# Four of the projections of a two-block network as units of seven block products, with one gate parked in DRAM

## The chip, the cores and the metric

The kernel runs on one core of a Trainium2 chip. The metric is the device time of one execution in microseconds (us). Engines are called as the profile calls them: PE (TensorE matmuls), PEld (its weight loads), DVE (VectorE), ACT (ScalarE), POOL (GpSimd) and SP (SyncE, which issues DMAs here).

## What is computed

Two blocks follow one another on x of 1024 positions by 1024 channels, in float32. Only two places bear on the change. The first mixer ends with an output projection:

```
x = x + concatenate([a, r]) @ w_out
```

The second mixer takes six slices of one projection and mixes two branches (each of the four D x D slices below, and w_conv_out, is a 1024 by 1024 by 1024 product):

```
proj = xn @ w_in + b_in
u_ssm, c_bgate, c_cgate, c_val, g_ssm, g_conv = split(proj)
z    = gelu(s5_branch(u_ssm))                       # 512 wide
y_a  = (z @ w_glu_a) * sigmoid(z @ w_glu_b)
y_b  = (c_bgate * causal_short_conv(c_cgate * c_val, conv_w, conv_b)) @ w_conv_out
merged = sigmoid(g_ssm) * y_a + sigmoid(g_conv) * y_b
h = h + merged @ w_out
```

After it stands an MLP with a hidden width of 4096 (squared relu) and a last norm.

## The kernel before

**Numbers.** A float32 operand is cut in two parts, high and low, and each product is three matmuls: high by high, high by low, low by high. ACT makes a high part with a copy (`make_high` line 513, or `high_a`, `high_w` lines 2069 and 2077), DVE the low part with a subtraction (`make_low` line 517, `low_a`, `low_w` lines 2085 and 2091). A matmul has 128x128 weights and 512 columns.

**project()** is the plain way to multiply. A list of jobs is cut into pieces of two k-tiles. For each piece SP loads the weights, ACT and DVE cut them (two pieces may be cut ahead), PE multiplies them into 8 (or 4) PSUM banks, and the last piece of a job is emptied by ACT or DVE with what the job asks for (a bias and a sigmoid, a multiplication, an addition). A product of 1024 by 1024 by 1024 takes 8 x 2 x 8 x 3 = 384 matmuls. Beside it runs a `side`: an object whose `vector`, `scalar`, `tensor` and `sync` methods are called once per piece and put other work into the engines' queues, by a share of costs per piece (`Side.turn`). A `following` list lets the first piece of the next stage be loaded and cut before the stage ends.

**Sevens** multiplies a list of units. A unit is one 1024 by 1024 by 1024 product, cut in blocks of 512, done as seven block products of sums (table `PRODUCTS`) in place of eight: 7 x 48 = 336 matmuls. It runs in 14 pieces (two halves for each product) of 24 matmuls. The sums of activations are made by DVE (`sum`); the sums of weights are made by the DMA engines: SP loads a block into a slot (line 2042), and POOL issues loads that add further blocks to it (`load_more`, line 2047), each waiting for the one before. For each product, `take` adds the PSUM banks to the blocks that they belong to (line 2150, DVE) or copies the first of them (ACT). `square` closes a block of the MLP's hidden layer. The sum T2 is the first that needs two additions in a row (`first_sums`), and its piece is the fifth.

**The stages around the change**, each a block of instructions with a barrier of all engines at its end: in the first mixer `mix_out` (two jobs of `project`, line 2402 reloads x beside it, and `MemoryTurned` norms and turns the memory rows); in `mix_second`, after the norm and the state-space input, `m2_cv` (the two value slices, with the recurrence beside it), `m2_gates` (slices 0 and 4 and then w_conv_out, with the short convolution beside it), `m2_last` (slice 3, into the buffer of x, with the gelu of the state-space output beside it), `m2_glu` (two 512-wide products) and then `mlp`, a Sevens of nine units (w_out and the MLP). The cross attention's output, `x_out`, is a Sevens of one unit.

## Time and profile before

| | us |
|---|---|
| median of the runs (3) | 3289.81 |
| lowest and highest | 3289.38, 3291.3 |
| the profiled execution, its own time | 3289.8 |
| its span in the profile | 3288.0 |
| PE busy (matmuls) | 2982.7 |
| DVE busy | 1706.5 |
| ACT busy | 1072.1 |

The profiled execution's time is the median of the runs. A span is from the first to the last instruction. PE is the engine with the largest busy share over the whole program; the shares by stage are in the rows below.

### The profile page before, as it was taken

To read this page: it belongs to the slowest core of one execution; us is meant where nothing else is said; L and a number is where in the kernel's file an instruction comes from. 1 tells how busy PE (TensorE), PEld (TensorE's weight loads), DVE (VectorE), ACT (ScalarE), POOL (GpSimd) and SP (SyncE) were. 2 spreads that over 40 slices of the span, in tenths; PEclk is the share of its full clock that TensorE was granted. 3 is DMA by queue.
4 is the path that set the end of the run, shared out by engine and by line. 5 is a ranking of instruction groups with operands and counts; after the bars stand their busy time and mean duration, and the time that the engine had idled before them with its cause. 6 is when DMAs were issued, how large, how long until landed. Compare 5 with 4: busy or idle time off the path is not lost. (4 is left out here: it accounts for less than half of the span.)

```text
span 3288.0 us, 36352 instructions
## 1 busy us (share of the span) xinstructions
PE 2982.7 (91%) x14320; PEld 2230.5 (68%) x14320; DVE 1706.5 (52%) x2382; ACT 1072.1 (33%) x1596; POOL 309.6 (9%) x347
## 2 busy tenths in 40 slices
PE   7998777999999889877776699999999999999998
PEld 7887754656878577332222688788888788888887
DVE  4125855886253675111110863752122778787878
ACT  3442334665143441100000422102132264434344
POOL 0001012210000000111110200000000011111110
PEclk8998888999999999999998799999999999999999
DMA  3121100002131238999996423211114455656663
GB/s 99 45 52 11 11 14 1 1 1 82 60 122 59 41 68 350 419 420 421 418 414 258 184 65 56 75 51 51 39 42 119 135 114 122 122 120 127 125 132 92
DMA packets 167418, 422.50 MB, mean 128 GB/s; under 512 B 47505, under 2 KB 61457, under 8 KB 141137
## 3 DMA queue, kind: packets, MB, share of 16 engines
q1 hardware_dynamic: 129696, 346.97, 29.3%
q0 software_dynamic: 36416, 69.23, 11.3%
q10 hardware_dynamic: 1152, 4.19, 0.3%
q8 instruction: 104, 1.70, 0.2%
q14 instruction: 50, 0.40, 0.0%
HBM read 405.13 MB, written 32.83 MB: 133 GB/s over the span
## 5 line engine op out<-in xcount | busy, mean ns | idle before, releaser
L2187 PE MATMUL mlp_ps<-mlp_w_ring,mlp_a_ring 128*128 128x512 f32 x1680 | 384.1, 390 | 4.2 <-PEq L572 4.2
L2187 PEld LDWEIGHTS mlp_ps<-mlp_w_ring,mlp_a_ring 128*128 128x128 f32 x1680 | 315.9, 188 | 70.1 <-issue 4.6
L2187 PE MATMUL mlp_ps<-mlp_a_ring,mlp_w_ring 128*128 128x512 f32 x1344 | 306.4, 389 | 1.3 <-ACT mlp_normed L4554 1.3
L3400 PE MATMUL ffn_ps<-moe_wgu,moe_rowsT 128*64 128x512 f32 x1024 | 244.9, 634 | 51.4 <-issue 26.9
L2187 PEld LDWEIGHTS mlp_ps<-mlp_a_ring,mlp_w_ring 128*128 128x128 f32 x1344 | 252.0, 188 | 53.7 <-issue 1.5
L517 DVE TENSOR_TENSOR m_w_cut<-m_w_raw,m_w_cut 128x512 fp32r<-128x512 f32 (+1 forms) x79 | 72.2, 914 | 363.1 <-ACT m_w_cut L513 362.8
L2077 ACT ACTIVATE mlp_w_ring<-mlp_raw 128x1024 fp32r<-128x1024 f32 x126 | 133.6, 1060 | 341.3 <-PE mlp_ps L2187 330.3
L3436 DVE TENSOR_TENSOR moe_hid<-ffn_ps,moe_gated 128x256 f32<-128x256 f32 x32 | 13.6, 425 | 416.0 <-ACT moe_gated L3448 416.0
L2091 DVE TENSOR_TENSOR mlp_w_ring<-mlp_raw,mlp_w_ring 128x1024 fp32r<-128x1024 f32 x126 | 154.2, 1224 | 115.4 <-ACT mlp_w_ring L2077 115.0
L3400 PEld LDWEIGHTS ffn_ps<-moe_wgu,moe_rowsT 128*64 128x64 f32 x1024 | 79.2, 145 | 196.4 <-issue 169.0
L513 ACT ACTIVATE m_w_cut<-m_w_raw 128x512 fp32r<-128x512 f32 (+1 forms) x79 | 64.0, 810 | 435.4 <-PE m_gates_ps L628 190.7
L628 PE MATMUL m_cv_ps<-m_high,m_w_cut 128*128 128x512 f32 x512 | 161.9, 398 | 7.0 <-DVE m_w_cut L517 2.9
L628 PE MATMUL m_gates_ps<-m_high,m_w_cut 128*128 128x512 f32 x512 | 157.8, 389 | 1.1 <-PEq L572 1.1
L2047 POOL DMA_DIRECT2D mlp_raw<-in_w_ff_dram x80 | 96.9, 1355 | 522.8 <-DMA mlp_raw<-in_w_ff_dram 320.7
L3421 PE MATMUL ffn_logitsT_ps<-moe_wd,moe_hidT 128*64 128x512 f32 x512 | 116.9, 598 | 18.2 <-DVE moe_hidT L3442 18.2
L517 DVE TENSOR_TENSOR mix_w_cut<-mix_w_raw,mix_w_cut 128x512 fp32r<-128x512 f32 (+1 forms) x47 | 31.4, 667 | 191.2 <-ACT mix_w_cut L513 191.1
L628 PE MATMUL mix_in_ps<-mix_high,mix_w_cut 128*128 128x512 f32 x384 | 118.7, 390 | 0.1
L628 PEld LDWEIGHTS m_cv_ps<-m_high,m_w_cut 128*128 128x128 f32 x512 | 95.8, 190 | 30.1 <-DVE m_w_cut L517 8.1
L3448 ACT ACTIVATE moe_gated<-ffn_ps 128x256 f32<-128x256 f32 x32 | 12.3, 384 | 315.4 <-PE ffn_ps L3400 315.4
L628 PE MATMUL mix_in_ps<-mix_w_cut,mix_high 128*128 128x512 f32 (+1 forms) x384 | 111.3, 372 | 0.9 <-PEq L286 0.9
L628 PEld LDWEIGHTS m_gates_ps<-m_high,m_w_cut 128*128 128x128 f32 x512 | 96.0, 188 | 21.4 <-issue 1.5
L2150 DVE TENSOR_TENSOR x<-x,mlp_ps 128x512 f32<-128x512 f32 x160 | 100.4, 683 | 5.8 <-PE mlp_ps L2187 5.8
(580 smaller groups left out, 5991.5 us busy)
## 6 DMA issues: line engine op xcount, KB each, us to landing
moe_wgu<-in_moe_w_gate_dram SPq DMA_DIRECT2D x64, 1024.0 KB, 19.2
moe_wgu<-in_moe_w_up_dram SPq DMA_DIRECT2D x64, 1024.0 KB, 24.6
moe_wd<-in_moe_w_down_dram SPq DMA_DIRECT2D x64, 1024.0 KB, 25.7
mlp_raw<-in_w_ff_dram POOLq DMA_DIRECT2D x80, 512.0 KB, 6.3
mlp_raw<-in_w_ff_dram SPq DMA_DIRECT2D x64, 512.0 KB, 3.8
m_w_raw<-in_w_in_dram SPq DMA_DIRECT2D x48, 256.0 KB, 2.8
mix_w_raw<-in_w_in_dram SPq DMA_DIRECT2D x40, 256.0 KB, 2.6
m_w_raw<-in_w_in_dram SPq DMA_DIRECT2D x20, 512.0 KB, 3.7
```

The source lines that it names most:

```text
L513: nc.scalar.activation(part(s, 0).bitcast(F32R), raw(s), ACT.Copy).then_inc(high_ready, 1)
L517: nc.vector.tensor_tensor(part(s, 1).bitcast(F32R), raw(s), part(s, 0), ALU.subtract).then_inc(low_ready, 1)
L628: ins = nc.tensor.matmul(ps[:, place, :r.shape[-1]], l, r, start=(k == 0 and sw is high and wh == 0), stop=(k == job.nk - 1 and sw is low))
L2047: pool.dma_start(self.slots[slot][:, 2 * h:2 * h + 2], self.block_of(u, name, h), accum_op=ALU.add).then_inc(self.more[slot][h], 16)
L2077: self.nc.scalar.activation(self.w_part(g, 0).bitcast(F32R), self.w_slot(name, h), ACT.Copy).then_inc(self.w_high, 1)
L2091: self.nc.vector.tensor_tensor(self.w_part(g, 1).bitcast(F32R), self.w_slot(PRODUCTS[q][1], h), self.w_part(g, 0), ALU.subtract).then_inc( ...
L2150: nc.vector.tensor_tensor(at, at, ps, ALU.subtract if q in NEGATIVE else ALU.add).then_inc(self.added, 1)
L2187: ins = self.nc.tensor.matmul(self.ps[:, 4 * banks + tile], l, r, start=(opens and h == k == n == 0), stop=(h == k == 1 and n == 2), skip_ ...
L3400: ins = self.nc.tensor.matmul(self.ps_h[r, i].rearrange("p (i n) -> p i n", i=2), self.rowsT[:, i, k, r], self.wgu[:, w * self.parts + h, ...
L3421: ins = self.nc.tensor.matmul(self.ps_y[r, half], self.hidT[:, i, k, r], self.wd[:, w * self.parts + h, k, half * CH:(half + 1) * CH], sta ...
L3436: self.nc.vector.tensor_tensor(self.hid[:, b % self.small], self.ps_h[:, b % self.small, EH:], self.gated[:, b % self.small], ALU.mult).th ...
L3448: self.nc.scalar.activation(self.gated[:, b % self.small], self.ps_h[:, b % self.small, :EH], ACT.Silu).then_inc(self.gated_ready, 1)
```

## The change

Of `m2_gates` nothing stays in `project`: slices 4 and 0 and w_conv_out become three units of a new Sevens, `gates`. Slice 3 (`m2_last`) now comes ahead of them, straight after `m2_cv`; its result leaves for DRAM in four parts (`gate_kept`), because the units use its buffer. Gelu's result, cut in high and low (`z_pair_kept`), goes to DRAM too, since its place is needed. The normed input is put together again from its parts (`normed`). Beside `m2_last` run gelu, the short convolution and this addition. The sigmoid of slice 4 is parked in DRAM in four blocks (`sigmoid_kept`) and comes back into `mixed`; z and the gate come back for `m2_glu`. `mix_out` becomes a Sevens of one unit (`mixed_out`), with the reload of x in four blocks and the memory rows' turning inside it. The first piece of `mlp` is now cut inside `m2_glu`'s last job (`FirstPiece` as a side), not behind it. `hold_sem` semaphores are given back (`release`), and buffers of `mlp` lie elsewhere.

```diff
@@ Sevens
-    def square(self, dve, u, q):
-        block = [b for b, first in TAKES[q] if not first][0]
...
+    def close(self, eng, u, q):
+        for block in [b for b, first in TAKES[q] if not first]:
+            for h in range(2):
+                eng.wait_ge(self.added, self.adds[self.at(u, q)] + 2 * h + 2)
+                self.units[u].close[1](eng, block, h).then_inc(self.made, 1)
@@ run, scalar, where nothing was cut ahead
+                        if not self.started:
+                            self.high_a(act, g)
                         self.high_w(act, g)
-                        self.high_a(act, g)
+                        if self.started:
+                            self.high_a(act, g)
...
+                        if g and h == 0:
+                            was, q_was, _ = self.piece(g - 1)
+                            if units[was].close[0] == "scalar":
+                                self.close(act, was, q_was)
@@ mix_first
-            project(c, "mix_out", stream, jobs, source=hT, fetch=fetch, side=turned, tail=turned, following=kv_jobs,
-                    busy=(28, 8))
+        mixed_out(c, a, x, hT, first_home - 4 * KD * T, kv_jobs).run()
+class MemoryBeside(Beside):
+    def fetch(self, sp):
+        rows = self.a["x"][0].rearrange("(m p) d -> p m d", p=P)
+        sv = self.sevens
+        sv.begin(sp)
+        for block, sem in self.back.items():
...
+            sp.dma_start(self.x[at], rows[at]).then_inc(sem, 16)
+            if block == "11":
+                sp.wait_ge(sv.more[2][1], 32)
+                for h in range(2):
+                    sv.load(sp, 0, "B22", 3, h)
+    def tensor(self, pe, g, tile):
+        sv = self.sevens
+        if (g, tile) in ((12, 1), (12, 3)):
+            m = tile // 2
+            pe.wait_ge(sv.added, sv.added_by(0, 4, 7))
+            self.turned.turn(pe, m)
+    def opening(self, pe):
+        self.c.keep_busy(self.turned.tail_ps[:, 0], 28)
@@ the side of m2_last
+class LastGate(Gelu):
+    def vector_steps(self, dve):
+        yield from super().vector_steps(dve)
+        yield from self.convolve()
+        while self.piece < 12:
+            yield None
+        dve.wait_ge(self.z_kept, 32)
+        for k in range(KD):
+            self.c.nc.vector.tensor_tensor(self.normed[:, k], self.pair[0][:, k], self.pair[1][:, k],
+                                           ALU.add).then_inc(self.restored, 1)
+            yield 1.3
+    def keep_gate(self, sp, j):
+        sp.wait_ge(self.emptied["scalar"], 4 * (j + 1))
+        at = slice(2 * j, 2 * j + 2)
+        sp.dma_start(self.kept_gate[:, at], self.gate[:, at]).then_inc(self.gate_kept[j], 16)
@@ beside the three units
+class GatesBeside(Beside):
+    def after_loads(self, sp, u):
+        sv = self.sevens
+        if u == 1:
+            for block in FINAL:
+                sp.wait_ge(sv.made, sv.final_done(0, block, 1))
...
+                sp.dma_start(self.kept_sigmoid[at], self.gate[at]).then_inc(self.sigmoid_kept[block], 16)
+        else:
+            for block in FINAL:
+                sp.wait_ge(self.sigmoid_kept[block], 16)
+            sp.wait_ge(sv.a_low, sv.split(1, "A22", 1))
+            sp.dma_start(self.mixed[:], self.kept_sigmoid).then_inc(self.sigmoid_back, 16)
+    def sync(self, sp):
...
+        self.stream.begin(sp, self.jobs)
+        sp.wait_ge(sv.made, sv.final_done(2, "21", 1))
+        for j in range(2):
+            at = slice(4 * j, 4 * j + 4)
+            sp.dma_start(self.gate[:, at], self.last.kept_gate[:, at]).then_inc(self.gate_back[j], 16)
+    def gpsimd_end(self, pool):
+        sv = self.sevens
+        pool.wait_ge(sv.a_low, sv.split(2, "A22", 1))
+        for part, kept in zip(self.z, self.last.kept_z):
+            pool.dma_start(part[:].bitcast(F32R), kept.bitcast(F32R)).then_inc(self.z_back, 16)
@@ mix_second
             project(c, "m2_u", stream, input_job, side=parameters, following=value_jobs, busy=(0, 9))
-            project(c, "m2_cv", stream, value_jobs, banks=4, side=Recurrence(s5, parameters), following=gate_jobs)
-            project(c, "m2_gates", stream, gate_jobs, side=conv, following=last_jobs)
+            project(c, "m2_cv", stream, value_jobs, banks=4, side=Recurrence(s5, parameters), following=last_jobs)
             c.recycle(0)
-            project(c, "m2_last", stream, last_jobs, banks=4, side=Gelu(c, u[:], z, *z_pair), following=glu_jobs)
-            sevens = out_and_mlp(c, a, x, t1, residual, moved, base)
-            project(c, "m2_glu", stream, glu_jobs, fetch=sevens.begin, tail=FirstPiece(sevens))
...
+            glu_jobs[0].ready = (gates.beside.z_back, 32)
+            project(c, "m2_last", stream, last_jobs, banks=4, side=last)
+            gates.run()
+            c.recycle(0)
+            sevens = out_and_mlp(c, a, x, mixed, residual, moved, base)
+            project(c, "m2_glu", glu_stream, glu_jobs, fetch=sevens.begin, side=FirstPiece(sevens, 6, 8))
             sevens.run()
@@ gate_units: what closes a block of each unit
+    def sigmoid(act, block, h):
+        chs, t = units[0].half(block, h)
+        for ch in range(chs.start, chs.stop):
+            ins = nc.scalar.activation(gate[:, ch, t], gate[:, ch, t], ACT.Sigmoid, bias=bias[:, 4, ch:ch + 1])
+        return ins
+    def times_conv(dve, block, h):
+        chs, t = units[1].half(block, h)
+        for ch in range(chs.start, chs.stop):
+            ins = nc.vector.scalar_tensor_tensor(conv[:, ch, t], gate[:, ch, t], bias[:, 0, ch:ch + 1],
+                                                 conv[:, ch, t], ALU.add, ALU.mult)
+        return ins
+    def times_sigmoid(dve, block, h):
+        chs, t = units[2].half(block, h)
+        dve.wait_ge(beside.sigmoid_back, 16)
+        return nc.vector.tensor_tensor(mixed[:, chs, t], mixed[:, chs, t], gate[:, chs, t], ALU.mult)
@@ FirstPiece, called at piece 6 of m2_glu
+    def scalar(self, act, s):
+        sv = self.sevens
+        if s == self.at:
+            sv.high_w(act, 0)
+            act.wait_ge(sv.w_low, 1)
+            act.wait_ge(self.emptied["vector"], self.before)
+            sv.high_a(act, 0)
```

**The order that results.** First DVE in the stage `m2_last`, before (its 16 pieces of weights are cut in the rows of `m_w_cut`; `m_u_cut` are the low parts of gelu's result):

```order
L517 TENSOR_TENSOR m_w_cut<-m_w_raw,m_w_cut 128x2x256 x4
L3972 TENSOR_TENSOR m_u_cut<-m_last_side_ps,m_t_cut 128x512 x2
...
L3972 TENSOR_TENSOR m_u_cut<-m_last_side_ps,m_t_cut 128x512 x2
L517 TENSOR_TENSOR m_w_cut<-m_w_raw,m_w_cut 128x2x256 x8
L453 TENSOR_TENSOR m_w_cut<-m_w_raw,m_w_cut 128x1024
```

and DVE in the same stage with the change, from the seventh piece's cut on (`m_conv` is the short convolution):

```order
L4010 TENSOR_TENSOR m_u_cut<-m_last_side_ps,m_t_cut 128x512 x2
L4621 TENSOR_SCALAR m_conv<-m_t,m_laid 128x1024
L4624 SCALAR_TENSOR_TENSOR m_conv<-m_t,m_laid,m_conv 128x1023
L523 TENSOR_TENSOR m_w_cut<-m_w_raw,m_w_cut 128x2x256
L4624 SCALAR_TENSOR_TENSOR m_conv<-m_t,m_laid,m_conv 128x1022
L4621 TENSOR_SCALAR m_conv<-m_t,m_laid 128x1024
L4624 SCALAR_TENSOR_TENSOR m_conv<-m_t,m_laid,m_conv 128x1023
L4624 SCALAR_TENSOR_TENSOR m_conv<-m_t,m_laid,m_conv 128x1022
L523 TENSOR_TENSOR m_w_cut<-m_w_raw,m_w_cut 128x2x256
```

The 24 operations of the convolution, which stood beside `m2_gates`, now stand three or four at a time between two cuts of `m2_last`, and 8 additions to `m_normed` follow them; the cut for the stage behind is gone.

Then ACT from the last job of `m2_last` into the next stage, with the change:

```order
L519 ACTIVATE m_w_cut<-m_w_raw 128x2x256 x3
L4613 ACTIVATE x<-m_last_ps,m_laid 128x512 x4
L578 UNCONDITIONAL_BRANCH
L2263 UNCONDITIONAL_BRANCH
L2090 ACTIVATE gates_a_ring<-m_normed 128x1024
L2098 ACTIVATE gates_w_ring<-gates_raw_15059 128x1024
```

Both high parts of the first piece stand behind the barrier (the two branches); before, the last cut in `m2_last` was the next stage's first piece.

Last SP, from the loads of the third unit to the end of the stage `gates`, and POOL's queue at the same place:

```order
L2063 DMA gates_raw_15061<-in_w_conv_out_dram 128x2x512 x2
L4106 DMA m_mixed<-sigmoid_kept 128x8192
L433 DMA m_glu_w_raw<-in_w_glu_b_dram 128x2x512 x2
L4116 DMA x<-gate_kept 128x4096 x2
L2235 UNCONDITIONAL_BRANCH
```

```order
L2068 DMA gates_raw_15059<-in_w_conv_out_dram 128x2x512 x2
L2068 DMA gates_raw_15061<-in_w_conv_out_dram 128x2x512 x2
L2068 DMA gates_raw_15062<-in_w_conv_out_dram 128x2x512 x2
L4122 DMA glu_z_high<-z_pair_kept 128x4096
L4122 DMA glu_z_low<-z_pair_kept 128x4096
L2235 UNCONDITIONAL_BRANCH
```

These five large loads (4 MB of sigmoids, 4 MB of gates, 4 MB of z) are new, and so are the stores that they read.

## Rows read from the trace of the kernel before

**Rows 1.** Page: busy time and share of the span; PE's granted clock in 40 slices.

```profile
PE 2982.7 (91%) x14320; PEld 2230.5 (68%) x14320; DVE 1706.5 (52%) x2382; ACT 1072.1 (33%) x1596; POOL 309.6 (9%) x347
...
PEclk8998888999999999999998799999999999999999
```

**Rows 2.** Windows: start:end length, busy us (count) PE PEld DVE ACT POOL, clock, DMA, GB/s.

```profile
811.30:898.60 87.30, 87.30 (x386) 72.26 (x387) 30.23 (x34) 17.35 (x21) 0.00 (x0) 1.00 0.29 107
2133.00:2395.20 262.20, 262.19 (x1152) 216.07 (x1152) 85.85 (x87) 44.36 (x49) 0.00 (x0) 1.00 0.16 47
2396.30:2488.60 92.30, 91.10 (x416) 75.17 (x416) 19.97 (x24) 34.96 (x43) 0.00 (x0) 1.00 0.18 52
1144.50:1221.10 76.60, 76.40 (x336) 62.98 (x336) 60.84 (x70) 33.51 (x43) 7.22 (x6) 1.00 0.31 56
2739.00:2893.00 154.00, 154.00 (x681) 127.50 (x680) 123.26 (x129) 65.84 (x73) 25.39 (x21) 1.00 0.62 126
2581.00:2585.00 4.00, 3.87 (x11) 3.15 (x12) 2.98 (x3) 3.83 (x4) 2.40 (x2) 0.63 0.79 266
```

**Rows 3.** Timeline at mix_out's end: start us, us, engine, line, [idle before <-releaser].

```profile
898.42 1.91 PE L2507 MATMUL mix_out_ps<-ident,x_mem 128*128 128x128 f32 x16
898.62 0.69 DVE L2421 TENSOR_TENSOR x<-mix_out_ps,x 128x512 f32<-128x512 f32 x1 [0.67 <-PE mix_out_ps L628]
...
904.18 0.47 PE L628 MATMUL x_kv_up_ps<-x_w_cut,x_memT 128*128 128x512 f32 x1 [0.30 <-PEq L572]
```

**Rows 4.** Timeline from m2_last into m2_glu.

```profile
2488.59 0.69 ACT L4451 ACTIVATE x<-m_last_ps,m_laid 128x512 f32<-128x512 f32 x1 [0.67 <-PE m_last_ps L628]
...
2489.58 0.70 PE L628 MATMUL m_glu_ps<-m_t_cut,m_w_cut 128*128 128x512 f32 x2 [1.03 <-PEq L572]
```

**Rows 5.** Lines in two units of mlp: busy us, mean ns | idle before.

```profile
L2091 DVE TENSOR_TENSOR mlp_w_ring<-mlp_raw,mlp_w_ring 128x1024 fp32r<-128x1024 f32 x28 | 34.3, 1224 | 28.1 <-ACT mlp_w_ring L2077 28.0
L2077 ACT ACTIVATE mlp_w_ring<-mlp_raw 128x1024 fp32r<-128x1024 f32 x29 | 30.8, 1061 | 81.6 <-PE mlp_ps L2187 81.6
...
L2150 DVE TENSOR_TENSOR x<-x,mlp_ps 128x512 f32<-128x512 f32 x32 | 20.1, 682 | 0.8 <-PE mlp_ps L2187 0.8
...
L2160 DVE SCALAR_TENSOR_TENSOR mlp_hidden<-mlp_hidden 128x1024 f32<-128x1024 f32 x8 | 9.4, 1221 | 0.0
```

**Rows 6.** Timeline from m2_glu into mlp.

```profile
2577.67 0.69 DVE L4508 TENSOR_TENSOR m_t<-m_t,m_glu 128x512 f32<-128x512 f32 x1
2578.28 1.22 DVE L2091 TENSOR_TENSOR mlp_w_ring<-mlp_raw,mlp_w_ring 128x1024 fp32r<-128x1024 f32 x1
2579.41 1.22 DVE L2085 TENSOR_TENSOR mlp_a_ring<-m_t,mlp_a_ring 128x1024 fp32r<-128x1024 f32 x1
...
2581.13 0.76 PE L2187 MATMUL mlp_ps<-mlp_w_ring,mlp_a_ring 128*128 128x512 f32 x1 [4.22 <-PEq L572]
```

**Rows 7.** Timeline of POOL: the additions of T2 beside m2_glu.

```profile
2494.45 2.59 POOL L2047 DMA_DIRECT2D mlp_raw<-in_w_out_dram  x2 [483.23 <-DMA mlp_raw<-in_w_out_dram]
2505.06 1.20 POOL L2047 DMA_DIRECT2D mlp_raw<-in_w_out_dram  x1 [8.02 <-DMA mlp_raw<-in_w_out_dram]
```

**Rows 8.** DMA issues of 2480 to 2680 us: size, median us to landing.

```profile
mlp_raw<-in_w_out_dram POOLq DMA_DIRECT2D x10, 512.0 KB, 9.9
...
x<-residual SPq DMA_DIRECT2D x2, 2048.0 KB, 11.2
```

**Rows 9.** DMA issues in two units of mlp.

```profile
mlp_raw<-in_w_ff_dram POOLq DMA_DIRECT2D x21, 512.0 KB, 6.3
```

**Rows 10.** Timeline of DVE in m2_last: the last cut of weights of a piece.

```profile
2478.43 0.69 DVE L517 TENSOR_TENSOR m_w_cut<-m_w_raw,m_w_cut 128x512 fp32r<-128x512 f32 x1 [4.75 <-ACT m_w_cut L513]
```

**Rows 11.** Lines of 1900 to 2500 us: the short convolution.

```profile
L4461 DVE SCALAR_TENSOR_TENSOR m_t<-m_t,m_laid 128x1023 f32<-128x1023 f32 (+1 forms) x16 | 20.5, 1284 | 0.6
...
L4459 DVE TENSOR_SCALAR m_t<-m_t,m_laid 128x1024 f32<-128x1024 f32 x8 | 6.5, 810 | 0.1
```

**Rows 12.** DMA issues of 1940 to 2110 us: a large store.

```profile
s_kept<-x SPq DMA_DIRECT2D x1, 2304.0 KB, 7.0
```

331 lines of the change are left out of this document (205 added, 126 removed).

## The prediction

> **What bounds the kernel now.** I read the page first, then windows over the stages that the change touches, then the timelines at their borders. On the page PE is busy 91% of the span at close to its full clock [rows 1]; the reader should see that no other engine has half as dense a record over the whole, so a stage is priced by PE until something in it is shown to be later. The windows say it for each stage [rows 2]: m2_gates (262.2 us for 1152 matmuls) and mix_out (87.3 us) have no idle time on PE at all, m2_last 1.2 us in 92.3, and DVE fills a third of the first two and a fifth of m2_last. So in these stages time is the number of matmuls by 262.2 / 1152 = 0.2276 us. The same view holds the price of what they become: the single unit of x_out took 76.6 us for its 336 matmuls (0.228 us each), and two units in the middle of mlp ran 154.0 us without a gap, with DVE at 123 of 154 us (80%) and the clock at 1.00. A unit is thus bound by PE too, with a fifth of DVE's time left. That is the whole case for a gain: fewer matmuls at the same rate. Against it stand the borders between stages, and DMAs that did not exist.
>
> **The change, part by part.**
>
> *Products, second mixer.* Six jobs of 192 matmuls become three units of 336: 1152 - 1008 = 144 fewer, by 0.2276 = **-32.8 us**. Slice 3 and the glu products keep their count.
>
> *Products, first mixer.* 384 become 336: 48 fewer, **-10.9 us**; the window of x_out against that of mix_out says 76.6 against 87.3 [rows 2], the same within 0.2.
>
> *mix_out's end.* Before, PE's last product ends at 898.6 and the next stage starts at 904.18 [rows 3]: 5.6 us, of which 1.9 are the 16 transposes of the memory rows, the rest a chain ACT, DVE, filler matmuls, barrier. Now the transposes stand inside the unit (1.9 again), and behind the last product come one addition (0.69), one cut of the next weights (1.22) and the barrier (0.3, below): 2.2. So 4.1 in place of 5.6: **-1.5 us**. Its start I leave as it is, since 28 filler matmuls stand ahead in both.
>
> *m2_last into gates.* Stages of `project` follow one another in 1.03 us: ACT's last emptying is 0.69, from 2488.59 to 2489.28, and PE begins 0.30 later [rows 4]; 0.30 is the barrier. The first piece of gates isn't cut ahead. Behind the barrier ACT makes two high parts (1.06 each) and DVE, after the second, a low part (1.22) [rows 5]: 0.7 + 0.3 + 2.1 + 1.2, and 0.5 for SP's last store of the gate, which is issued after the last emptying, and for semaphores: 4.8 us. Against 1.0: **+3.8 us**.
>
> *gates into m2_glu.* After the last product: one addition 0.68, two closings of 1.22 (the multiplications by the conv branch's sigmoid, 1024 elements, as L2160), one cut for m2_glu 1.22 [rows 5], barrier 0.3, semaphores 0.2: 4.8 us against 1.1: **+3.7 us**.
>
> *m2_glu into mlp.* Before, two cuts of 1.22 stood between DVE's last addition and the barrier, and PE idled 4.22 us [rows 6]. They move ahead of the last job's emptying, where DVE has room: the gap falls to about 1.8, **-2.4 us**.
>
> *The clock at these borders.* After that 4.22 us gap, the 4 us from 2581 to 2585 have a granted clock of 0.63 [rows 2], a mean of the two levels: most of it was at the lower one (1.2 GHz), the rest at 2.4; 4 x 0.37 = 1.5 us lost. Gaps of 1.0 us leave it at full. So the two new gaps of 4.8 cost 1.5 each, and the one that shrinks to 1.8 gives its 1.5 back: **+1.5 us**. If the clock doesn't fall, this is 0 or -1.5; if both new stages start a whole 4 us at the lower level, +2.5.
>
> *T2 of the first unit.* In mlp the unit's first weight sum was begun in the stage ahead; in gates and mix_out it begins with the stage. Beside m2_glu the chain ran like this: stage begin 2489.5, first addition issued at 2494.45, the second, which waits for it, at 2505.06 [rows 7], 15.5 us after the begin, and landed 6.3 [rows 9] to 9.9 us [rows 8] later: 21.8 to 25.4, with the two cuts 24.1 to 27.7. PE wants it for the fifth piece: 3.5 us to start, four pieces of 24 x 0.2276 = 5.46, 1.5 for the clock, so at 26.8. I take **+0.4 us**, between 0 and 3 (the stage starts with 3 MB of other loads and a 1 MB store, much as m2_glu did). In mix_out PE starts 7.3 us after the begin, which leaves 3 us over: 0, at most 3.
>
> What a rule says of this: the Trainium skill, in "DMA: Bandwidth & Descriptors", section "SWDGE vs HWDGE vs iDMA", states that an engine serves the software and hardware queues in turn. By it an addition beside a busy SP queue would take twice the 6.3 us, and T2 would be later by 3 us than I take, each time it starts with a stage. The trace has 9.4 us for the first of them (2494.45 + 1.2 to 2505.06), half of the way there, so I keep the row.
>
> *z, for m2_glu.* POOL issues the two loads of 2 MB when the low part of the last A22 is made, about 12.5 us before the last product's end (three pieces less two cuts). The nearest rows are two loads of the same size in flight together, 11.2 us each [rows 8]: z is there 0 to 1 us after the last product, PE starts 4.8 after it: **0**. Bound from above: at the pace of POOL's 512 KB additions, two in flight in 6.3 us, 4 MB take 25 us and PE waits 9. The copy row is nearer, since nothing is added here. The skill's fit in "Anatomy of one DMA" (2.0 us + bytes / 436e3, same page) gives 6.8 us for each load, 11.6 for both if they share the engines; by it the wait is 0 as well and the upper bound falls away.
>
> *The 4 MB at each unit's border.* The sigmoid blocks are stored as the first unit ends, and come back as the second ends. SP's loads of blocks stand ahead of them in its queue, so only additions on POOL's queue share the engines. There the two units of mlp show DMA at 0.62 with 126 GB/s [rows 2]; 4 MB are some 11 us of it at the rate of rows 8. T2 of an inner unit has some 14 us of room (its second addition goes out before the unit starts). Cost 0 to 3 each; I take **+1.5 us** for both and for the x blocks in mix_out.
>
> *DVE in m2_last.* The 24 operations of the convolution (1.284 and 0.81 us [rows 11]) and 8 additions (1.22) come to DVE, 37 us to the 20 of before. At most four stand between two cuts: 3 x 1.284 + 0.81 + 0.69 for the cut [rows 10] = 5.35 us against PE's 5.46 for a piece, and a cut has another 4 us before PE wants it. **0.** If each group took 0.3 longer it would eat that room in 13 pieces, and there are 7: still 0. The additions wait for the stores of z: 2304 KB took 7.0 us [rows 12], two of 2 MB have 25. Moved, not added, otherwise: 16 splits of the conv result (8 ACT, 8 DVE) go, which lay under PE.
>
> **Sum.** -32.8 - 10.9 - 1.5 + 3.8 + 3.7 - 2.4 + 1.5 + 0.4 + 1.5 = -36.7. The profiled execution's own time, 3289.8, is the median: **3253 us**.
>
> **The rivals.**
>
> *The parked data and the late sums hold PE.* Each bound above comes true in part: z late by up to 9, T2 by 3 in both places, the borders inside gates by 3 each. For it: in 2581 to 2585 the DMAs were already at 0.79, and rows 7 show an addition at 9.4. Against it: no unit of mlp or x_out waited on a weight. Half of the bounds' 21 us gives 3263; all of them 3274. Chance 0.22.
>
> *DVE paces m2_last.* For it: 5.35 of 5.46 us is no margin, and a chained operation waits for its own semaphore. Against it: 57 us in a stage of 92. If every one of 12 pieces came 0.7 us late: 3261. Chance 0.06.
>
> *Slower than before: the weight sums set the pace in all four units.* One mechanism: an addition's landing. A unit's T2 needs two in a row, with 14 us of room inside gates and about none at the two starts. It costs nothing at 6.3 to 9.9 us a landing. At 7.9 us each (the mean of 9.4 and 6.3) the first unit's T2 is about on time, so at L us a unit that starts a stage loses 2 x (L - 7.9) and an inner one 14 less. For two of each that is 8 x (L - 7.9) - 28, which reaches 36.7 at L = 16: from there the gain is gone. At 20 us it is 69, and 3289.8 - 36.7 + 69 = 3322. It decides in POOL's queue. Against it: 9.9 is the largest median of the trace, in the stretch with the densest DMAs. Chance 0.03.
>
> *The change doesn't do what it says.* The order shows 336 matmuls for each new unit; what could fail is that something equal in size is given back, 30 us or more by small waits at 42 + 14 new pieces. Time as before. Chance 0.03.
>
> *Everything is hidden.* No clock loss, no late sum, borders at 4 us: -32.8 - 10.9 - 1.5 + 3 + 3 - 2.4 - 1.5 = -43, 3247. Chance 0.1; the forecast's own case, 3248 to 3258, has the rest, 0.56.
>
> **How the numbers follow.** The likeliest case gives 3253. The range has to leave out no more than 2 in 10: from 3247, where all is hidden, to 3270, most of the way through the first rival. About 0.2% (6.6 us) is what a measurement of this kernel can tell from no change. Faster by more than that are all cases but the last two named and a sliver of the first rival: 0.93; within it 0.03; slower 0.04.
>
> **What would show it.** Right: 1008 matmuls in gates within 230 to 233 us of PE without a wait, 336 in mix_out in 76.5 plus 1.9 of transposes; gaps before gates and m2_glu of 4.5 to 5 us, each followed by a clock below 1.00, and one below 2 us before mlp. Wrong: PE waits for DVE's or ACT's cut of a weight in the fifth piece of a unit (T2), an idle PE at m2_glu's first matmul released by a DMA of z, additions of POOL with landings above 12 us, or gaps between the pieces of m2_last.

## The result and the profile after

| | before | after |
|---|---|---|
| median of 6 runs, us | 3288.74 (3287.44 to 3291.3) | 3263.72 (3259.24 to 3274.4) |
| profiled execution, us | 3289.8, span 3288.0 | 3268.3, span 3266.5 |
| matrix products and transposes on PE | 14320 | 14128 |
| mean granted clock | 0.965 | 0.960 |

The ratio is 0.9925, 95% interval 0.991 to 0.9941: 25 us less. The forecast was 3253, 36.7 less, with 3247 to 3270 around it. So the sign and the range held, and a third of the expected gain is missing. The page's first two parts, of after (against [rows 1]):

```profile
PE 2951.9 (90%) x14128; PEld 2201.6 (67%) x14128; DVE 1862.9 (57%) x2542; ACT 1159.9 (36%) x1707; POOL 362.6 (11%) x389
...
PEclk8999888999999999999999699999999999999999
```

PE lost 192 instructions and 31 us of busy time; the span lost 21.5. Where the rest went is read stage by stage. The start of each stage's first product stands in the view of its PSUM tile (the memory bank that the products are added up in); the differences make this table (us, profiled executions):

| stretch | before | after | change | forecast |
|---|---|---|---|---|
| last product of attention to first of mix_out | 8.8 | 7.8 | -1.0 | 0 |
| mix_out, to the next stage's first product | 92.9 | 90.2 | **-2.7** | -12.4 |
| m2_cv | 227.2 | 228.6 | +1.4 | 0 |
| m2_gates and m2_last, now m2_last and gates, to m2_glu's first product | 356.6 | 333.3 | -23.3 | -23.4 |
| m2_glu, to mlp's first product | 91.5 | 97.5 | **+6.0** | -0.9 |
| mlp, first to last product | 697.2 | 695.8 | -1.4 | -1.5 |

(Forecast of the fourth row: -32.8 + 3.8 + 3.7 + 1.5 for the clock at the head of gates + 0.4; of the fifth: -2.4 + 1.5. The 1.5 for the 4 MB stands in no row.) The rest of the span, code that the change doesn't touch, adds -0.5. Two rows hold the miss: mix_out and m2_glu. The windows of after, in the columns of [rows 2]: mix_out; m2_last; gates; m2_glu; the first 4 us of gates and of m2_glu; of mlp.

```profile
808.90:896.90 88.00, 81.05 (x357) 66.48 (x356) 62.44 (x71) 30.85 (x34) 12.30 (x10) 0.96 0.64 173
2130.20:2223.10 92.90, 91.44 (x416) 75.06 (x416) 54.13 (x55) 33.91 (x41) 0.00 (x0) 1.00 0.37 130
2228.10:2459.00 230.90, 230.87 (x1008) 190.54 (x1008) 170.22 (x175) 117.99 (x146) 37.63 (x32) 0.99 0.70 177
2463.50:2559.10 95.60, 91.08 (x384) 74.40 (x384) 40.07 (x55) 17.81 (x25) 4.85 (x4) 0.96 0.42 130
...
2228.00:2232.00 4.00, 3.87 (x9) 3.10 (x10) 2.35 (x3) 0.52 (x1) 0.92 (x1) 0.50 0.99 373
2463.00:2467.00 4.00, 3.55 (x8) 2.81 (x9) 1.36 (x2) 1.06 (x1) 0.00 (x0) 0.50 1.00 360
2561.00:2565.00 4.00, 3.99 (x18) 3.33 (x19) 3.07 (x3) 3.74 (x4) 2.39 (x2) 1.00 0.85 279
```

gates is as forecast: 1008 products without a gap in 230.9 us. m2_last takes 92.9 with 54 us on DVE. But mix_out, with 336 products and 16 transposes, takes 88.0 and is idle for 7 of them, and m2_glu, whose products the change leaves alone, takes 95.6 instead of 87.3 and is idle for 4.5. The first 4 us of gates and of m2_glu have a granted clock of 0.50, the lower of the two levels (1.2 GHz); those of mlp have 1.00.

**mix_out.** PE's long idle stretch, and what ACT did before it (timeline of after: start us, us, engine, line, [idle before <-releaser]), then the loads on SP's queue, then (second fence) the sizes and landings in 795 to 880 us and SP's own wait there:

```profile
868.96 13.21 PE L2208 MATMUL mix_out_ps<-mo_w_ring,mo_a_ring 128*128 128x512 f32 x47 [5.36 <-issue]
...
861.40 1.06 ACT L2588 ACTIVATE x_mem_junk<-x_mem 128x1024 f32<-128x1024 f32 x1 [12.07 <-DMA x_gains<-in_norm_cross_dram]
...
865.43 1.04 ACT L2098 ACTIVATE mo_w_ring<-mo_raw 128x1024 fp32r<-128x1024 f32 x1
...
829.20 5.85 SPq L2471 DMA_DIRECT2D x<-in_x_dram  x3
835.09 0.60 SPq L2564 DMA_DIRECT2D x_mem<-in_mem_dram  x1
835.74 10.72 SPq L2564 DMA_DIRECT2D x_gains<-in_norm_mem_dram  x1
846.50 1.97 SPq L2564 DMA_DIRECT2D x_gains<-in_norm_cross_dram  x1
```

```profile
mo_raw<-in_w_out_dram POOLq DMA_DIRECT2D x10, 512.0 KB, 9.6
...
x<-in_x_dram SPq DMA_DIRECT2D x4, 1024.0 KB, 19.4
x_mem<-in_mem_dram SPq DMA_DIRECT2D x1, 1024.0 KB, 23.3
...
SPq L2063 <- DMA mo_raw<-in_w_out_dram: 22.0, 1, 22.0
```

ACT takes the memory rows' norms at piece 7 and waits 12.07 us for the rows and gains. They were asked for at 835 to 848, behind four blocks of x, and landed at 861. Behind that wait, on ACT, stands the high part of the next weights (865.43): PE runs dry for 5.36 us. In the kernel before the same rows were asked for at 805 to 807 and landed some 17 us later, more than 30 us before ACT took their norms at 856.1 (before: SP's timeline, a landing, ACT's line in the view of `x_mem`):

```profile
805.48 0.58 SPq L2457 DMA_DIRECT2D x_mem<-in_mem_dram  x1
...
x_gains<-in_norm_cross_dram SPq DMA_DIRECT2D x1, 512.0 KB, 17.8
...
L2481 ACT ACTIVATE x_mem_junk<-x_mem x2: 1043/1044/1044, 856.1 to 858.8; 128x1024 f32<-128x1024 f32 x2
```

The larger part of the delay is not the 4 MB themselves. Behind the first block of x, SP stood for 22.0 us at a wait for the weight sum T2 (`sp.wait_ge(sv.more[2][1], 32)` in the diff), and the other blocks of x and the rows stand behind that wait in SP's program. The bytes and SP's slow issues add the rest: one of the two gain loads alone took SP 10.72 us. This is read from the trace; no run here takes SP's wait away by itself.

**m2_glu.** A like pattern, with another load (timeline of after: PE, ACT, SP's queue; last line, SP at the same six blocks in the kernel before):

```profile
2492.05 1.22 PE L634 MATMUL m_glu_ps<-glu_z_high,m_glu_w_cut 128*128 128x512 f32 x2 [4.51 <-DVE m_glu_w_cut L523]
...
2489.68 1.06 ACT L519 ACTIVATE m_glu_w_cut<-m_glu_w_raw 128x1024 fp32r<-128x1024 f32 x1 [25.19 <-DMA m_glu_w_raw<-in_w_glu_b_dram]
...
2462.03 0.81 SPq L4116 DMA_DIRECT2D x<-gate_kept  x2
2463.41 10.18 SPq L2063 DMA_DIRECT2D mlp_raw<-in_w_out_dram  x6
2473.63 2.30 SPq L433 DMA_DIRECT2D m_glu_w_raw<-in_w_glu_b_dram  x2
...
2489.53 3.51 SPq L2042 DMA_DIRECT2D mlp_raw<-in_w_out_dram  x6
```

The parked gate (2 x 2 MB) comes back over SP's queue at 2462.03, straight ahead of six blocks for mlp. SP then needs 10.18 us to issue those six (3.5 before the change), the third weight piece of m2_glu is issued at 2473.6 and is there 16 us later, and PE waits 4.51 us for its cut. The 4 us from 2492 have a granted clock of 0.61.

**The borders**, gates into m2_glu (timeline of DVE and PE):

```profile
2459.04 0.69 DVE L2173 TENSOR_TENSOR x<-x,gates_ps 128x512 f32<-128x512 f32 x1 [0.67 <-PE gates_ps L2208]
2459.65 2.35 DVE L4738 TENSOR_TENSOR m_mixed<-m_mixed,x 128x1024 f32<-128x1024 f32 x2
2461.92 1.22 DVE L459 TENSOR_TENSOR m_glu_w_cut<-m_glu_w_raw,m_glu_w_cut 128x1024 fp32r<-128x1024 f32 x1
...
2463.45 1.19 PE L634 MATMUL m_glu_ps<-glu_z_high,m_glu_w_cut 128*128 128x512 f32 x2 [4.45 <-PEq L2235]
```

The chain is the one of the forecast, 4.45 us for 4.8. The gap ahead of gates is 5.02 for 4.8, and that ahead of mlp 1.9 for 1.8 (timeline of PE in after):

```profile
2228.13 34.13 PE L2208 MATMUL gates_ps<-gates_a_ring,gates_w_ring 128*128 128x512 f32 x140 [5.02 <-DVE gates_w_ring L2112]
...
2561.01 4.33 PE L2208 MATMUL mlp_ps<-mlp_w_ring,mlp_a_ring 128*128 128x512 f32 x18 [1.92 <-PEq L578]
```

### The profile page after: what moved, and what is told of

It reads as the page before. It is cut to its first block and busy times, and to the rows that moved or that the text cites. A ratio compares the mean times of both kernels' runs of the same rounds, so it can differ in the third digit from the quotient of the medians.

```text
span 3266.5 us, 36538 instructions
## 1 busy us (share of the span) xinstructions
PE 2951.9 (90%) x14128; PEld 2201.6 (67%) x14128; DVE 1862.9 (57%) x2542; ACT 1159.9 (36%) x1707; POOL 362.6 (11%) x389
## 5 line engine op out<-in xcount | busy, mean ns | idle before, releaser
L2208 PE MATMUL gates_ps<-gates_a_ring,gates_w_ring 128*128 128x512 f32 x1008 | 230.9, 392 | 5.0 <-DVE gates_w_ring L2112 5.0
L2208 PEld LDWEIGHTS gates_ps<-gates_a_ring,gates_w_ring 128*128 128x128 f32 x1008 | 190.5, 189 | 45.4 <-DVE gates_w_ring L2112 5.4
L634 PEld LDWEIGHTS m_cv_ps<-m_high,m_w_cut 128*128 128x128 f32 x512 | 96.2, 191 | 31.2 <-DVE m_w_cut L523 7.8
L523 DVE TENSOR_TENSOR m_w_cut<-m_w_raw,m_w_cut 128x512 fp32r<-128x512 f32 (+1 forms) x49 | 35.5, 724 | 135.0 <-ACT m_w_cut L519 134.6
L634 PE MATMUL m_cv_ps<-m_low,m_w_cut 128*128 128x512 f32 x256 | 101.2, 395 | 0.0
```

Source lines behind the costliest of these rows:

```text
L523: nc.vector.tensor_tensor(part(s, 1).bitcast(F32R), raw(s), part(s, 0), ALU.subtract).then_inc(low_ready, 1)
L634: ins = nc.tensor.matmul(ps[:, place, :r.shape[-1]], l, r, start=(k == 0 and sw is high and wh == 0), stop=(k == job.nk - 1 and sw is low))
L2208: ins = self.nc.tensor.matmul(self.ps[:, 4 * banks + tile], l, r, start=(opens and h == k == n == 0), stop=(h == k == 1 and n == 2), skip_ ...
```

## The experiments

Twelve kernels on four chips, each against the kernel before on the same chip. In the table a ratio stands with its 95% interval; the three stage columns (us, from the profiled execution, as in the table above) carry the verdicts, because the code between the first mixer's input and the end of attention, which no kernel here touches, ended anywhere from 791.4 to 803.4 us in these profiles and so hides a few microseconds in a whole time. Each stage column rests on one profile. How far such a number can be trusted shows where the code of a stage is the same: m2_last and gates took 333.0 to 333.4 us in the six kernels that only differ elsewhere (and 334.8 in old_mix, below), m2_glu 96.2 to 97.8, or 91.3 to 91.5 with the gate late, but mix_out anything from 81.0 to 83.0, by a wait of 0.3 to 2.2 us at piece 12.

| kernel | median us | ratio | mix_out | m2_last + gates | m2_glu |
|---|---|---|---|---|---|
| changed kernel | 3263.7 | 0.9925 (0.991 to 0.9941) | 90.2 | 333.3 | 97.5 |
| gate_late | 3256.8 | 0.9898 (0.9878 to 0.9918) | 89.5 | 333.0 | 91.4 |
| rows_late | 3254.5 | 0.9898 (0.9879 to 0.9916) | 81.4 | 333.4 | 97.8 |
| both_late | 3249.9 | 0.9878 (0.986 to 0.9896) | 81.0 | 333.1 | 91.3 |
| old_mix | 3267.7 | 0.9937 (0.9918 to 0.9956) | 92.9 | 334.8 | 96.2 |
| held | 3251.1 | 0.9887 (0.9867 to 0.9907) | 81.6 | 336.4 | 89.2 |
| first_after | 3255.3 | 0.9902 (0.9884 to 0.992) | 83.0 | 333.2 | 94.8 |
| mem_first | 3258.2 | 0.9913 (0.9897 to 0.9929) | 85.6 | 333.2 | 91.5 |
| best | 3251.5 | 0.9888 (0.9868 to 0.9908) | 82.8 | 336.6 | 89.2 |
| held15 | 3249.3 | 0.99 (0.9884 to 0.9917) | 81.3 | 335.1 | 89.2 |
| gate_pool | 3262.7 | 0.9934 (0.9918 to 0.9951) | 81.0 | 346.3 | 91.8 |
| best2 | 3255.4 | 0.9908 (0.9891 to 0.9924) | 85.9 | 335.7 | 89.3 |
| held_end | 3249.3 | 0.9891 (0.9874 to 0.9907) | 81.8 | 333.7 | 89.2 |

### gate_late: the gate comes back behind m2_glu's weights

```diff
 class GatesBeside: def sync(self, sp):
         self.stream.begin(sp, self.jobs)
-        sp.wait_ge(sv.made, sv.final_done(2, "21", 1))
-        for j in range(2):
...
-            sp.dma_start(self.gate[:, at], self.last.kept_gate[:, at]).then_inc(self.gate_back[j], 16)
 class FirstPiece:
+    def sync(self, sp, s):
...
+        if s in (0, 1):
...
+            sp.dma_start(g.gate[:, at], g.last.kept_gate[:, at]).then_inc(g.gate_back[s], 16)
```

> The changed kernel, only that the parked gate comes back (two halves of 2 MB) from inside m2_glu, behind the loads of m2_glu's weight pieces 2 and 3, instead of at the end of gates. Theory: PE's 4.5 us of waiting in m2_glu for the third weight piece come from the 4 MB that stand ahead of its load on SP's queue; then the wait goes, and with it the 2 us at the lower clock behind it: 6 to 7 us less than the changed kernel's median of 3263.7, so 3257 to 3258, and the piece lands within 10 us of its issue. Rival: z's loads, six blocks for the first unit of mlp and T2 fill the DMAs by themselves; then the piece is as late as before and the time within 1.5 us of 3263.7. Second rival: the gate now lands too late and DVE or PE waits for it: slower than 3263.7.

m2_glu's stretch fell from 97.5 to 91.4 us, 6.1 less, and PE has no idle stretch left in it. ACT now gets the third piece in time (timeline of ACT in gate_late):

```profile
2482.33 1.06 ACT L519 ACTIVATE m_glu_w_cut<-m_glu_w_raw 128x1024 fp32r<-128x1024 f32 x1 [17.27 <-DMA m_glu_w_raw<-in_w_glu_b_dram]
```

The piece still took some 14 us from its issue (2468.6), not the 10 expected. It is in time because it was issued 5 us sooner: two pieces of 10.9 us from PE's start at 2464.0, and 2 for the clock, make 2487.8 the time at which PE wants it, and it was cut at 2484.6. The gate itself landed a median of 22.5 us after its issue and nobody waited for it. So the gate's load, where it stood, made the wait, and the margin without it is small. Whether its place in the queue or its bytes did it, this run doesn't tell; gate_pool was to.

### rows_late: the memory rows' norms two pieces later

```diff
 class MemoryBeside: def scalar(self, act, g):
-        if g == 7:
+        if g == 9:
             self.turned.scalar(act, 4)
...
     def after_low(self, dve, g):
-        if g == 8:
+        if g == 10:
             self.turned.vector(dve, 5)
```

> The changed kernel, only that ACT takes the memory rows' norms at piece 9 of mix_out instead of 7, and DVE its share at 10 instead of 8. Theory: ACT stands for 12 us at the wait for the memory rows and gains, whose loads are queued behind 4 MB of x; the cut of the next weights is behind that wait, so PE stops 5.4 us and runs 4 us at half clock behind it. Two pieces are 10.9 us: the wait goes, 5.4 + 2.0 = 7 us less, 3256 to 3257. Rival: DVE, at 70% of mix_out, is behind as well, and the 1.6 us wait at piece 12 grows because the norms now stand nearer to the transposes: 3 us or less are won, 3261 or more.

mix_out's stretch fell from 90.2 to 81.4 us, 8.8 less, of which up to 2 can be the scatter named above. The 5.36 us wait went, and with it the low clock behind it (0.50 over 4 us and 0.89 over the next 4 in the changed kernel, some 2.4 us); of the 1.6 us at piece 12, 0.8 are left. The window of the stage in rows_late shows what the forecast had asked for, 78.4 us for the products and transposes, within 1:

```profile
801.90:881.20 79.30, 78.52 (x357) 64.93 (x356) 62.94 (x72) 31.56 (x35) 12.30 (x10) 1.00 0.72 190
```

### both_late: the two together

> Both edits together. The two stages are 1600 us apart, so the gains should add: 13 to 14 us less than the changed kernel, 3249.5 to 3251, if both theories hold. It should also scatter less than the changed kernel's runs (15 us from lowest to highest), if the two waits on DMAs are what varies from run to run; if it scatters as much, the cause of the scatter is elsewhere.

3249.9, and the two stages as in the single runs: they add. By the ratios, 0.9878 is 40 us off the kernel before, more than the 36.7 of the prediction's sum. The stages of the table, from the end of attention to mlp's last product, add up to 36.7 less than before in the two profiles; the same number is in part luck, since m2_cv's 1.3 us, which no term had, are in it. Most of the rest lies in code that the change doesn't touch: attention ended at 795.4 us for 802.5. The runs lay 5.8 us apart; but gate_late's were 12.5 apart, rows_late's 10.6 and held15's, which has both edits, 10.7, and the kernel before, which has neither wait, spread over 17.2 on the same chip. So that part of the expectation is not borne out. The end of attention, at 791.4 to 803.4 us in these profiles, is where most of the scatter can come from.

### old_mix: the second mixer's part alone

The end of mix_first is that of the kernel before (project with its 384 products, turned_after behind them); all else is the changed kernel.

> The changed kernel with mix_out as it was in the kernel before (384 products, through project), so the second mixer's part of the change alone. By the profiles the next stage starts 5.1 us sooner with the new mix_out: theory 3263.7 + 5 = 3269. By the step of the prediction (12.4 us) it would be 3276. Rival: the new mix_out also costs something later (buffers, semaphores), then it is 3265 or less.

3267.7: by the medians and by the ratios (0.9937 against 0.9925) the new mix_out was worth about 4 us in the changed kernel, not 12.4; the intervals overlap, and the stage says it more surely. Its stretch is 92.9 again, to the tenth, for 90.2. The 5.1 us of the expectation had counted in 1.4 us by which attention ended sooner, and 1.0 ahead of the stage's first product. Of the 1.5 us more in m2_last and gates, 0.9 are z's: it landed 15.7 us after its issue, and the gap ahead of m2_glu was 5.39 us for 4.45.

### mem_first: the rows ahead of x in the queue

```diff
 class MemoryBeside: def fetch(self, sp):
...
         sv.begin(sp)
+        self.c.memory.fetch(sp)
         for block, sem in self.back.items():
...
     def sync(self, sp):
-        self.c.memory.fetch(sp)
```

(on gate_late, norms at pieces 7 and 8)

> gate_late, with the memory rows and gains (2 MB) loaded ahead of the 4 MB of x in mix_out, and the norms left at pieces 7 and 8. Theory: the place in SP's queue alone made ACT wait 12 us; now the rows land about 15 us after their issue at 806, at 822, and ACT never waits for them: the 5.4 us wait and its clock go as in both_late, 3250. Rival: the x block for the first additions or the last weight blocks, now behind 2 MB more, come late (x landed 19 us after its issue already): PE waits 2 to 5 us in the first half of mix_out, 3252 to 3255.

3258.2, slower than either side of the expectation had it, and no better than gate_late's 3256.8. The stage took 85.6, halfway between gate_late's 89.5 and both_late's 81.0. The theory's first half came true, since ACT never waited for the rows; but so did the rival, since PE stood once, earlier (timeline of PE and of ACT in mem_first):

```profile
824.55 48.13 PE L2208 MATMUL mix_out_ps<-mo_w_ring,mo_a_ring 128*128 128x512 f32 x204 [3.32 <-issue]
...
820.22 1.06 ACT L2098 ACTIVATE mo_w_ring<-mo_raw 128x1024 fp32r<-128x1024 f32 x1 [13.26 <-DMA mo_raw<-in_w_out_dram]
```

This is T2: its additions share the engines with 2 MB more (POOL waited 8.28 us for the first, against 6.42 in the changed kernel), and the summed weights are there 3.3 us too late. The clock fell to 0.57 behind it. In this stage the DMAs have no slack at the start; a load moved forward pushed another one onto the path. Moving the wait on ACT cost nothing in rows_late; moving the load forward did here.

### first_after: the first piece of mlp cut behind m2_glu again

```diff
-            project(..., side=FirstPiece(sevens, 6, 8, gates.beside))
+            project(..., side=FirstPiece(sevens, None, 8, gates.beside))
```

(on both_late)

> both_late, only that the first piece of mlp is cut behind the last emptying of m2_glu again, as in the kernel before, instead of at piece 6 beside it. Theory (two steps of the prediction): the gap ahead of mlp grows from 1.9 to 4.2 or more (ACT's two high cuts now stand there too: up to 6) and 1.5 to 2 us of clock go behind it: 3.9 to 6 us more than both_late, 3254 to 3256. Rival: the gap ahead of mlp is hidden by other work, within 1 us of both_late.

As the theory has it (timeline of PE in first_after):

```profile
2545.52 4.61 PE L2208 MATMUL mlp_ps<-mlp_w_ring,mlp_a_ring 128*128 128x512 f32 x10 [5.40 <-PEq L578]
```

The gap ahead of mlp is 5.4 for 1.9, which makes m2_glu's stretch 94.8 for 91.3, and mlp takes 698.2 for 695.8, with a granted clock of 0.50 in its first 4 us: 5.9 us together, and 5.4 in the medians. This small part of the change is worth more than the whole new mix_out was in the changed kernel.

### held, best, held15, held_end: the clock at the two heads

```diff
 class GatesBeside:
+    def opened(self, ps):
+        self.ps = ps
+    def opening(self, pe):
+        self.c.keep_busy(self.ps[:, 0], N)
+    def tensor_end(self, pe):
...
+        pe.wait_ge(sv.copied, sv.copies[sv.at(2, 5)])
+        pe.wait_ge(sv.added, sv.adds[sv.at(2, 5)])
+        self.c.keep_busy(self.ps[:, 0], N)
```

(on both_late; N is 30 in held, 15 in held15, and in held_end 15 without the opening. `keep_busy` issues small products that nobody reads, fillers.)

> both_late with 30 small filler products on PE as gates opens (3.5 of its 5.0 us gap) and 30 behind the last product of gates (3.5 of the 4.4 us gap). Theory: the 4 us at half clock at the head of gates and of m2_glu come from the idle PE ahead of them; with fillers the granted clock there is 1.00 and 2.0 us come back at each: 4 us less than both_late, 3246, and no other stage moves. Rival: the clock falls there whatever PE does (a heavy start of the DMAs, DVE and ACT together): time within 1 us of both_late, or up to 1 us longer if the last filler holds back the first real product.

The clock was held: 21 products in the first 4 us of gates at 1.00, where the changed kernel had 9 at 0.50 (windows of held at the head of gates):

```profile
2218.30:2222.30 4.00, 4.00 (x21) 3.32 (x20) 0.17 (x1) 1.26 (x2) 2.59 (x2) 1.00 1.05 408
```

But keep_busy(30) is 60 instructions and 6.9 us, twice what I had counted, and PE was late by the fillers themselves: m2_last and gates took 336.4 for 333.1. m2_glu, at full clock, took 89.2 for 91.3, and mlp 697.5 for 695.8. The median of 3251.1 is not below both_late's.

> held with half the fillers. In held each filler product took two instructions of 0.115 us, so 30 of them took 6.9 us, 2 to 3 us longer than the gaps, and gave back what the clock gained. 15 take 3.45 us, inside both gaps (5.0 and 4.4 us, of which about 1 us of each lies on the far side of the barrier). Theory: the gaps stay at 5.0 and 4.4, the first 4 us of gates and of m2_glu run at a granted clock of 1.00 instead of 0.50, 2.0 us come back at each: stages m2_last and gates together 331.1 for 333.1, m2_glu with its gap 89.3 for 91.3, time 3246. Rival: the 1 us without work that is left in each gap is enough for the clock to fall: nothing is won, 3250.

m2_glu as expected, 89.2 for 91.3. gates not: it started at full clock and then stood at the fifth piece (timeline of PE and ACT in held15, and windows over the 8 us behind the stop):

```profile
2236.80 8.47 PE L2208 MATMUL gates_ps<-gates_a_ring,gates_w_ring 128*128 128x512 f32 x29 [2.17 <-issue]
...
2233.24 1.06 ACT L2098 ACTIVATE gates_w_ring<-gates_raw 128x1024 fp32r<-128x1024 f32 x1 [8.86 <-DMA gates_raw<-in_w_in_dram]
...
2236.80:2240.80 4.00, 4.00 (x13) 3.16 (x14) 3.92 (x4) 1.93 (x3) 0.53 (x2) 0.69 1.13 205
2240.80:2244.80 4.00, 4.00 (x17) 3.27 (x16) 4.00 (x6) 2.39 (x4) 0.93 (x1) 0.88 1.10 188
```

T2 landed some 24 us after the stage's begin (2209), and with the clock held that is what the head of gates waits for. In the changed kernel PE was slow enough not to notice. The 2.17 us of waiting brought a lower clock of their own behind them (0.69 and 0.88, 1.7 us), so m2_last and gates took 335.1, 2 us more than in both_late: at this head the fillers cost time.

> both_late with 15 fillers behind the last product of gates alone. In held15 the clock at the head of gates was held, but PE then waited 2.2 us for T2 at the fifth piece, and the stage ended no sooner; at the head of m2_glu the clock was worth 2.1 us (89.2 for 91.3). Theory: T2's landing, 24 us behind the stage's begin, hides the slow clock at the head of gates, so leaving it slow there costs nothing: m2_last and gates take 333.1 us as in both_late, m2_glu with its gap 89.2, 2 us less than both_late (3249.9 on its chip), ratio to the kernel before 0.987. Rival: the fillers ahead of gates were what slowed gates in held15; that gives the same here, but then no PE wait for T2 would show in held15. Second rival: z, which landed 2.6 us ahead of the barrier, is later and takes the place of the gap: m2_glu starts no sooner, 91 us.

m2_glu's stretch is 89.2 again. But m2_last and gates took 333.7 for 333.1, and mlp 697.5 for 695.8, so the 2.1 us were given back in full: whole time 3249.3, not to be told from both_late. The 333.7 also bear out the theory's first part: with the slow clock left at the head of gates, 1.4 of the 2 us that held15 lost there are gone. Two things took the gain. First, z: it was issued at 2430.57 and landed 15.3 us later, at 2445.9, after DVE's last closing, and the stage began 1.6 us behind it (DVE was done at 2446.66, PE began at 2447.52). Second, the clock fell at mlp's head instead (windows of held_end and of both_late over the first 4 us of mlp, each behind a gap of 1.9 us). It did so in held, best and best2 too (0.60, 0.57, 0.65; mlp 697.4 or 697.5), but not in held15 (1.00):

```profile
2536.70:2540.70 4.00, 3.97 (x11) 3.16 (x12) 3.05 (x3) 3.76 (x4) 2.39 (x2) 0.57 0.80 274
```

```profile
2538.80:2542.80 4.00, 4.00 (x18) 3.29 (x19) 3.11 (x3) 3.71 (x4) 2.39 (x2) 1.00 0.80 270
```

best is held with one more edit: the first weight piece of m2_glu is cut at pieces 39 (ACT) and 40 (DVE) of gates.

> held, and the first weight piece of m2_glu is cut by ACT and DVE at pieces 39 and 40 of gates instead of behind the last product. Theory: DVE's chain behind the last product (addition 0.69, two closings 2.35, cut 1.22) loses the cut: 1.2 us less than held, 3245. Rival: DVE is the last at piece 40 and the cut delays an addition: no gain, or up to 1 us more.

3251.5, no gain, since held's fillers ran to the end of the gap anyway (PE was idle for 0.3 us ahead of m2_glu): a test that could show nothing.

### gate_pool: the 4 MB by POOL's queue

```diff
 class GatesBeside: def gpsimd_end(self, pool):
...
+        pool.wait_ge(sv.made, sv.final_done(2, "21", 1))
+        for j in range(2):
...
+            pool.dma_start(self.gate[:, at], self.last.kept_gate[:, at]).then_inc(self.gate_back[j], 16)
```

(on rows_late, without SP's two loads)

> rows_late, with the 4 MB of the gate loaded at the same moment as in the changed kernel, but by POOL's queue behind z instead of by SP's. It tells the place in the queue from the bytes. Theory (place in the queue): the third weight piece of m2_glu is no longer behind the 4 MB, PE does not wait in m2_glu, its stage takes 91.4 us instead of 97.8, time 3249 to 3250. Rival (bytes): 8.5 MB must pass in any case before the piece is whole, the piece lands at the same time, PE waits 4 us again, 3254 to 3256.

Neither: 3262.7. m2_glu itself took 91.8 without a wait, but PE stood 17.5 us ahead of it, 13 more than in the changed kernel (timeline of POOL, and the sizes and landings, in gate_pool):

```profile
2449.51 0.53 POOL L4122 DMA_DIRECT2D x<-gate_kept  x1 [0.25 <-issue]
```

```profile
x<-gate_kept POOLq DMA_DIRECT2D x1, 2048.0 KB, 11.7
```

All engines begin the next stage at 2462.9, 1.7 us behind the landing at 2461.2, though nothing in m2_glu wants the gate before its first job is done. So this stage did not end before the DMAs on POOL's queue had landed, though no line of the kernel waits for them there, while those on SP's queue passed over the border (the changed kernel's gate did). That the 4 MB had landed before the stage began also means that this run can't tell place from bytes. That question stays open.

### best2: three edits on held15

The cut of best; the memory rows and gains are loaded between the second and the third block of x, behind SP's wait for T2; the norms stand at pieces 8 and 9.

> held15, with the first weight piece of m2_glu cut at pieces 39 and 40 of gates (as in best), and with the memory rows and gains of mix_out loaded between the second and the third block of x, the norms at pieces 8 and 9. Theory: the cut is worth 1.2 us of the gap ahead of m2_glu; in mix_out ACT no longer waits for the rows, DVE's norms stand a piece further from the transposes, and the 0.3 to 2.1 us that PE waits at piece 12 go: 1.2 to 3 us less than held15, 3243 to 3245. Rival: the third and fourth block of x, now behind 2 MB, come late and DVE's additions with them: mix_out takes 82 us or more, nothing won.

The rival again: 3255.4, mix_out 85.9, PE waits 3.7 us for DVE's additions, and DVE for a block of x (timeline of DVE and PE in best2):

```profile
854.63 2.48 DVE L2173 TENSOR_TENSOR x<-x,mix_out_ps 128x512 f32<-128x512 f32 x4 [3.52 <-DMA x<-in_x_dram]
...
874.50 4.57 PE L2208 MATMUL mix_out_ps<-mo_w_ring,mo_a_ring 128*128 128x512 f32 x12 [3.68 <-DVE x L2173]
```

And the early cut still gained nothing, for another reason than in best: DVE was done at 2455.04, but z, issued at 2440.09 with 15.7 us to its landing, was there at 2455.8, and the stage began at 2457.4, 1.6 behind that.

## Why the forecast was right, and where it was not

- **Products of the second mixer, -32.8.** Right. 1008 products, 230.9 us, no wait; at 0.2276 us each they are 229.4, and 1.5 are the clock's. DVE at 170 of 231 us was no bound. The prediction opens with a misreading that changes nothing: DVE's 52% is more than half of PE's 91%.
- **Gaps of 4.8 and 4.8 us, and below 2 ahead of mlp.** Right: 5.0, 4.45, 1.9. first_after prices the last one, with its clock, at 5.9 us.
- **Products of the first mixer, -10.9, and its end, -1.5.** The step that failed: the prediction took 336 products at the pace of x_out and let the memory rows cost nothing. The count was right, the end was (2.2 us behind the last product, as taken), and rows_late shows the stage at 79.3. I compared the window of x_out with that of mix_out and so priced the products, but didn't ask, as I had to, what stands behind ACT's and DVE's waits for the memory rows. The change sends those rows behind SP's 22 us wait for T2 and behind 4 MB of x in four blocks, and leaves ACT's wait at piece 7. That cost 8.8 us (90.2 against 81.4).
- **The 4 MB at each border, +1.5.** The second step that failed: too small, and in the wrong place. No row showed the 1.5. The sigmoid's store and load inside gates cost PE nothing. The gate's 4 MB at the border to m2_glu I listed in the change, but not as a load ahead of six blocks and a weight piece on SP's queue; they cost 6.1 us (97.5 against 91.4). Whether by their place or by their bytes is open.
- **z, 0.** Right, with less to spare than thought: 9.3 and 13.5 us to landing, for 11.2 taken, so 2.8 us ahead of m2_glu's first product. With z at 15.3 and 15.7 (held_end; best2 and old_mix) it sets the border. The fit that the Trainium skill gives in "DMA: Bandwidth & Descriptors", section "Anatomy of one DMA", came to 11.6 us for both; the traces have 12.8 (gate_late) to 15.7 for the second load on this queue, so here the measurement decides.
- **T2, +0.4.** Right in time: ACT had the summed weights at 2248.45, 24 us behind the begin of gates (2224.5), inside the 21.8 to 25.4 of the rows. PE did not wait, so the 0.4 was 0. The extra 3 us that the Trainium skill's rule of serving the queues in turn would have made by the prediction's estimate ("DMA: Bandwidth & Descriptors", section "SWDGE vs HWDGE vs iDMA") were not there. The forecast had the form right: it counted the clock's 1.5 us into the time at which PE wants T2, and added only what is left of T2 behind them. held15 shows that the two run side by side: it took the clock's loss away, and T2's wait took its place.
- **The clock, +1.5.** Right in kind, a little small: 0.50 over the whole first 4 us at both new heads, 2 us each where 1.5 was taken (the +2.5 that the prediction names as its upper case), and 1.00 at mlp's. In mix_out and inside m2_glu the waits brought a low clock that no term had.
- **DVE in m2_last, 0.** Right: 54.1 us busy in 92.9, the stage 0.6 longer than before.
- **m2_cv**, untouched, took 1.4 us more. It did so in all but two of these kernels (228.3 to 228.6; 227.1 in held15, 227.2 in old_mix, as before). held and both_late, next to held15 in code, have 228.4 and 228.5, so no edit explains it, and it stays open.
- **The rivals.** The first one gave the time (3263 at half of its bounds) without being right: of z, T2 and the sigmoid's blocks, which it named, none held PE in the changed kernel. Two other loads did. That 3263.7 lies inside the range is in part luck: the room up to 3270 was given for waits that did not come, and two that nobody had listed filled it. The chance for a wait on a DMA was fair, the list of DMAs was not complete.

The best kernel here is both_late: by the medians 14 us, by the ratios 15 us under the changed kernel. held15 and held_end have the same median, with more code.

## What to carry to other kernels

Price a moved load not by its own landing alone, but by what stands behind it in its queue and by what stands behind the wait for it on the engine that waits; both misses were side work ahead of a weight piece in something that works in order, on ACT a wait for rows, on SP the loads of the gate. A wait on the engine that issues a load delays that load as surely as bytes ahead of it do. Where the wait is only in the wrong place, move the wait: two pieces later cost nothing here, while moving the load forward put T2 on the path. Delays at a stage's head (a slow clock, a late sum, a late reload) can run side by side, as in gates, so taking one away can show the next rather than its own price.
